# Stick-breaking heads taken two at a time, with the mask added by a matmul

## What is computed

```python
z = jnp.einsum('bhqd,bhkd->bhqk', qb, kh) * scale
valid = key_pos < qpos
log_keep = jnp.where(valid, jax.nn.log_sigmoid(-z), 0.0)
after = lax.cumsum(log_keep, axis=3, reverse=True) - log_keep
attn = jnp.where(valid, jnp.exp(jax.nn.log_sigmoid(z) + after), 0.0)
out = jnp.einsum('bhqk,bhkd->bhqd', attn, vh)
```

## Time and profile before

| | us |
|---|---|
| median of 3 runs | 1650.35 (1649.11 to 1651.74) |
| the profiled execution | 1655.24 |
| its span, first to last instruction | 1653.4 |
| TensorE busy | 1580.4 (96%) |
| VectorE busy | 1065.9 (64%) |
| ScalarE busy | 750.5 (45%) |
| Pool busy | 450.5 (27%) |

### The profile page before, as it was taken

One profiled execution on the slowest core, in us unless ns is written; L12 is line 12 of the kernel. 1 busy time (PEld: TensorE's weight loads), 2 busy tenths in 40 slices (PEclk: granted clock), 3 DMA queues, 4 the chain that ended last, 5 costly groups with the idle time before them and its releaser, 6 DMA issues. The chain is left out here.

```text
span 1653.4 us, 32293 instructions
## 1 busy us (share of the span) xinstructions
PE 1580.4 (96%) x11998; PEld 1514.0 (92%) x11998; DVE 1065.9 (64%) x1685; ACT 750.5 (45%) x1079; POOL 450.5 (27%) x180
## 2 busy tenths in 40 slices
PE   8999899998999998999999999999998899899997
PEld 7778899998999998888999999999998888899997
DVE  6233777755755549886875553655539886877863
ACT  5233555544544533246454443544443335554442
POOL 4224300053434410000244443334410000244452
PEclk9779999999999999899999999999999899999999
DMA  7212445662565534324455564556644333456563
GB/s 241 72 52 90 115 153 179 193 224 89 178 177 185 194 118 144 104 86 126 146 169 175 172 210 148 164 176 181 204 125 140 103 102 114 146 175 184 186 229 98
DMA packets 65834, 250.87 MB, mean 152 GB/s; under 512 B 7520, under 2 KB 8800, under 8 KB 65760
## 3 DMA queue, kind: packets, MB, share of 16 engines
q1 hardware_dynamic: 65760, 249.85, 49.1%
HBM read 248.77 MB, written 1.05 MB: 151 GB/s over the span
## 5 line engine op out<-in xcount | busy, mean ns | idle before, releaser
L335 POOL TENSOR_TENSOR wlo<-raw,whi 128x1024 fp32r<-128x1024 f32 (+1 forms) x168 | 442.7, 2637 | 1182.3 <-ACT whi L378 1182.3
L1131 PE MATMUL W<-xh,whi 128*128 128x272 f32 (+2 forms) x2416 | 708.8, 293 | 16.5 <-DVE wlo L664 13.4
L1133 PE MATMUL W<-xh,wlo 128*128 128x272 f32 (+2 forms) x2416 | 699.3, 289 | 0.0
L1132 PE MATMUL W<-xl,whi 128*128 128x272 f32 (+2 forms) x2416 | 697.8, 289 | 0.0
L378 ACT ACTIVATE whi<-raw 128x1024 fp32r<-128x1024 f32 (+1 forms) x439 | 483.5, 1107 | 138.1 <-PE W L1133 97.4
L1131 PEld LDWEIGHTS W<-xh,whi 128*128 128x128 f32 x2416 | 462.7, 192 | 25.2 <-issue 18.0
L1132 PEld LDWEIGHTS W<-xl,whi 128*128 128x128 f32 x2416 | 463.0, 192 | 0.5
L1133 PEld LDWEIGHTS W<-xh,wlo 128*128 128x128 f32 x2416 | 462.8, 192 | 0.0
L664 DVE TENSOR_TENSOR wlo<-raw,whi 128x1024 fp32r<-128x1024 f32 (+1 forms) x269 | 345.1, 1283 | 69.1 <-ACT whi L378 68.7
L1131 PE MATMUL W<-ah,whi 128*128 128x272 f32 (+2 forms) x1168 | 333.4, 285 | 8.7 <-DVE proj L1068 3.5
L1133 PE MATMUL W<-ah,wlo 128*128 128x272 f32 (+2 forms) x1168 | 332.2, 284 | 0.0
(11 more groups left out here) (159 smaller groups left out, 1083.6 us busy)
## 6 DMA issues: line engine op xcount, KB each, us to landing
raw<-in_w SPq DMA_DIRECT2D x359, 512.0 KB, 3.6
raw<-in_w SPq DMA_DIRECT2D x80, 704.0 KB, 4.1
h<-in_hT SPq DMA_DIRECT2D x4, 272.0 KB, 5.0
out<-h SPq DMA_DIRECT2D x4, 256.0 KB, 2.5
scr<-in_cst SPq DMA_DIRECT2D x1, 1000.0 KB, 9.2
cst<-in_cst SPq DMA_DIRECT2D x1, 408.0 KB, 6.6
prm<-in_prm SPq DMA_DIRECT2D x1, 180.0 KB, 8.7
m<-in_meta SPq DMA_DIRECT2D x1, 64.0 KB, 8.9
```

Source lines behind the costliest of these rows:

```text
L335: pool.tensor_tensor(wlo[:, j, 0:cols], raw[:, j, 0:cols], whi[:, j, 0:cols].bitcast(F32), ALU.subtract).then_inc(lo_ready[j], 1)
L1131: pe.matmul(out, whi[:, j, w], mh, start=start and k == 0, stop=False, skip_group_check=True)
L1132: pe.matmul(out, whi[:, j, w], ml, start=False, stop=False, skip_group_check=True)
L1133: ins = pe.matmul(out, wlo[:, j, w], mh, start=False, stop=stop and k == len(rhs) - 1, skip_group_check=True)
```

## The change

The eight heads become four pairs, one pair every four steps from step 14. Both heads of a pair have one pass each on ScalarE and VectorE, over 2 x 432 columns in two neighbouring PSUM banks (XP).

- `scores(c)`, step 14 + 4c: for each of the two banks first one fast matmul (identity by a constant with -1e30 at masked keys, 432 columns), then the three matmuls of each head, the two heads by turns: one on array rows 0 to 63, the other on 64 to 127.
- `soften(c)`, step 15 + 4c; `keeps(c)`, step 16 + 4c, is one pass, without the mask. `sums(c)`, step 16 + 4c, uses negated constants. `arguments` is gone; `weights(c)`, step 17 + 4c, reads PSUM. `values(c)`, step 17 + 4c, takes the heads by turns on columns 0 to 63 and 64 to 127.
- Taps: 4 a step before step 14, 6 from there on.
- The values are turned at step 12 and copied at steps 13 to 15.
- Pool makes the rounded copies of the identity and the mask once, at the start; the constants grow by 128 columns.

```diff
-for name, n in [("kpad", CC * 384), ("u", CC * (CONV_K - 1 + T)), ("y", CC * T), ("soft", SBW),
-                ("keep", SBW), ("attn", SBW)]:
+for name, n in [("kpad", CC * 384), ("u", CC * (CONV_K - 1 + T)), ("y", CC * T), ("keep", 2 * SBW),
+                ("attn", 2 * SBW)]:
     SC2[name] = (o, n)
     o += n
...
-        room = 0 if s < 2 else 4 if s < G_GLU else 5 if s % 2 or s <= SB_FROM else 6
+        room = 0 if s < 2 else 4 if s < SB_FROM else 6
...
-        cst = sb("cst", [P, 3 * P + SBW])
+        cst = sb("cst", [P, 4 * P + SBW])
+        identr, hider = sb("identr", [P, P], F32R), sb("hider", [P, SBW], F32R)
...
-        trige = cst[:, 2 * P:3 * P]
-        unseen = cst[:, 3 * P:3 * P + SBW]
+        minus_later, minus_ones = cst[:, 2 * P:3 * P], cst[:, 3 * P:4 * P]
+        hide = cst[:, 4 * P:4 * P + SBW]
...
-        soft, keep, attn = s2("soft"), s2("keep"), s2("attn")
+        keep, attn = (s2(x).rearrange("p (b n) -> p b n", b=2) for x in ("keep", "attn"))
...
-        X = [ctx.enter_context(nc.psum_tensor(f"X{i}", [P, 512], F32)) for i in range(4)]
+        XP = ctx.enter_context(nc.psum_tensor("XP", [P, 2, 512], F32))
+        X = [XP[:, 0, :], XP[:, 1, :]] + [ctx.enter_context(nc.psum_tensor(f"X{i}", [P, 512], F32))[:, :] for i in (2, 3)]
...
             for j in range(2, 4):
                 lo(0, j, S8)
+            pool.wait_ge(cst_landed, 16)
+            pool.tensor_copy(identr[:, :], ident).then_inc(hide_ready, 1)
+            pool.tensor_copy(hider[:, :], hide).then_inc(hide_ready, 1)
             los(N_QKV1 - 1, 1, K8A)
             los(N_WO, G_WO1, K8A)
             los(N_DN, G_DN1, K11)
...
             def mixer(g, l, p, t):
-                def soften(hd):
-
-                    n = 3 * (SB_H * l + hd)
-                    act.wait_ge(z_mm, SB_H * l + hd + 1)
-                    if hd:
-                        act.wait_ge(keep_ready, SB_H * l + hd)
-                    act.activation(soft, X[hd % 2][:, 0:SBW], ACT.Abs).then_inc(soft_step, 1)
+                def soften(c):
+
+                    n = 3 * (CC * l + c)
+                    act.wait_ge(z_mm, CC * l + c + 1)
+                    act.activation(keep, XP[:, :, 0:SBW], ACT.Abs).then_inc(soft_step, 1)
                     act.wait_ge(soft_step, n + 1)
-                    act.activation(soft, soft, ACT.Exp, scale=-1.0).then_inc(soft_step, 1)
+                    act.activation(keep, keep, ACT.Exp, scale=-1.0).then_inc(soft_step, 1)
                     act.wait_ge(soft_step, n + 2)
-                    act.activation(soft, soft, ACT.Ln, bias=1.0).then_inc(soft_step, 1)
-
-                def weights(hd):
-                    act.wait_ge(arg_ready, SB_H * l + hd + 1)
-                    act.activation(attn, attn, ACT.Exp).then_inc(attn_ready, 1)
+                    act.activation(keep, keep, ACT.Ln, bias=1.0).then_inc(soft_step, 1)
+
+                def weights(c):
+
+                    act.wait_ge(cum_mm, CC * l + c + 1)
+                    if c:
+                        act.wait_ge(o_mm, CC * l + c)
+                    act.activation(attn, XP[:, :, 0:SBW], ACT.Exp).then_inc(attn_ready, 1)
 
                 def out_hi(c):
-                    act.wait_ge(o_mm, SB_H * l + 2 * c + 2)
+                    act.wait_ge(o_mm, CC * l + c + 1)
                     act.activation(ah[:, c, :], X[2][:, 0:T], ACT.Copy).then_inc(o_hi, 1)
 
                 for s in range(4 * N_MIX):
-                    hd, late = divmod(s - SB_FROM - 1, 2)
-                    if not late and 0 <= hd < SB_H:
-                        soften(hd)
-                    if not late and 1 <= hd <= SB_H:
-                        weights(hd - 1)
-                    if not late and hd >= 3 and hd % 2:
-                        out_hi((hd - 3) // 2)
+                    c, phase = divmod(s - SB_FROM, 4)
+                    if phase == 0 and 1 <= c <= CC:
+                        out_hi(c - 1)
+                    if phase == 1 and 0 <= c < CC:
+                        soften(c)
+                    if phase == 3 and 0 <= c < CC:
+                        weights(c)
                     if s == LN_FROM + 3:
                         for c in range(CC):
                             act.wait_ge(ln_cent, CC * l + c + 1)
@@ -978,23 +984,10 @@
                             dve.scalar_tensor_tensor(y[:, c, :], u[:, c, k:k + T], w, y[:, c, :], ALU.mult,
...
-                def keeps(hd):
-
-                    n = SB_H * l + hd
-                    dve.wait_ge(soft_step, 3 * n + 3)
-                    if hd:
-                        dve.wait_ge(cum_mm, n)
-                    dve.scalar_tensor_tensor(keep, X[hd % 2][:, 0:SBW], 0.0, soft, ALU.max, ALU.add).then_inc(sp_step, 1)
-                    dve.wait_ge(sp_step, n + 1)
-                    dve.scalar_tensor_tensor(keep, unseen, 1.0, keep, ALU.subtract, ALU.mult).then_inc(keep_ready, 1)
-
-                def arguments(hd):
-
-                    n = SB_H * l + hd
-                    dve.wait_ge(cum_mm, n + 1)
-                    if hd:
-                        dve.wait_ge(o_mm, n)
-                    dve.scalar_tensor_tensor(attn, unseen, NEG, X[hd % 2][:, 0:SBW], ALU.mult, ALU.add).then_inc(arg_ready, 1)
+                def keeps(c):
+
+                    dve.wait_ge(soft_step, 3 * (CC * l + c) + 3)
+                    dve.scalar_tensor_tensor(keep, XP[:, :, 0:SBW], 0.0, keep, ALU.max, ALU.add).then_inc(keep_ready, 1)
 
                 def out_lo(c):
...
                     j, n = s % 4, 4 * g + s + 1
-                    hd, late = divmod(s - SB_FROM - 1, 2)
-                    if not late and 1 <= hd < SB_H + 1:
-                        arguments(hd - 1)
-                    if not late and 0 <= hd < SB_H:
-                        keeps(hd)
+                    pair, phase = divmod(s - SB_FROM, 4)
+                    if phase == 2 and 0 <= pair < CC:
...
                     else:
                         scaled(proj[:, GSB + s - G_QK, t:], j, n, t).then_inc(evac_done, 1)
                     lo_ahead(g + s // 4, j, K8D, K8D)
-                    if G_V + 2 < s <= G_V + 5:
-                        b = s - G_V - 3
+                    if G_V < s <= G_V + 3:
+                        b = s - G_V - 1
                         dve.wait_ge(v2_mm, 3 * l + b + 1)
...
                     taps(s)
-                    if not late and hd >= 3 and hd % 2:
-                        out_lo((hd - 3) // 2)
...
 
                 def attn_gate(j):
                     for m in (2 * j, 2 * j + 1):
@@ -1375,43 +1366,50 @@
 
...
             def mixer(g, l, t):
-                def scores(hd):
-
-                    c, p0, bank = hd // 2, 64 * (hd % 2), hd % 2
+                def scores(c):
+
                     pe.wait_ge(evac_done, 4 * g + G_V + 2 * c + 2)
-                    if hd == 1:
+                    if c == 0:
                         pe.wait_ge(v2_ready, 3 * l + 1)
-                    elif hd >= 2:
-                        pe.wait_ge(arg_ready, SB_H * l + hd - 1)
+                        pe.wait_ge(hide_ready, 2)
+                    else:
+                        pe.wait_ge(attn_ready, CC * l + c)
+                    for bank in range(2):
+                        mm(X[bank][:, 0:SBW], identr[:, :], hider[:, :], True)
                     for b in range(3):
                         a, w = P * b, T - P * b
-                        ins = mm(X[bank][:, SB_AT[b]:SB_AT[b] + w], kpad[p0:p0 + 64, c, a:a + P],
-                                 proj[p0:p0 + 64, QQ + c, a:T], b == 0)
+                        for bank in range(2):
+                            p0 = 64 * bank
+                            ins = mm(X[bank][:, SB_AT[b]:SB_AT[b] + w], kpad[p0:p0 + 64, c, a:a + P],
+                                     proj[p0:p0 + 64, QQ + c, a:T], False)
                     ins.then_inc(z_mm, 1)
...
-                def sums(hd):
-
-                    bank = hd % 2
-                    pe.wait_ge(keep_ready, SB_H * l + hd + 1)
-                    for b in range(3):
-                        for jb in range(b, 3):
-                            r = BLK[jb][1] - BLK[jb][0]
-                            w = T - P * jb
-                            ins = mm(X[bank][:, SB_AT[b] + P * (jb - b):SB_AT[b] + P * (jb - b) + w],
-                                     (trige if jb == b else ones)[0:r, :], keep[0:r, SB_AT[jb]:SB_AT[jb] + w], False)
+                def sums(c):
+
+                    pe.wait_ge(keep_ready, CC * l + c + 1)
+                    for bank in range(2):
+                        for b in range(3):
+                            for jb in range(b, 3):
+                                r = BLK[jb][1] - BLK[jb][0]
+                                w = T - P * jb
+                                ins = mm(X[bank][:, SB_AT[b] + P * (jb - b):SB_AT[b] + P * (jb - b) + w],
+                                         (minus_later if jb == b else minus_ones)[0:r, :],
```

(55 more changed lines are left out.)

## The result

| | before | after |
|---|---|---|
| median of 6 runs, us | 1648.27 | 1658.57 |
| ratio to before (95% interval) | | 1.0068 (1.005 to 1.0086) |
| profiled execution, us | 1655.24 | 1658.78 |
| its span, us | 1653.4 | 1656.9 |

A forecast was written before the change was run, and what follows sets the result against it. The prediction took TensorE to set the mixer's time, through its work, its waits for VectorE and its clock. Work and waits -6.6 us, clock +19.7, together +13.1 on 1650.35, gave 1663.5 us; range 1643 to 1677.

The forecast's parts named there:

- scores of a pair: TensorE in the mixer: two heads' scores side by side take 1.1 us, within bounds of 1.02 and 2.04.
- values of a pair: TensorE in the mixer: two heads' values side by side take 1.2 us, within bounds of 1.06 and 2.12.
- work per layer: TensorE's work in a layer's mixer: scores save 2.2 us and values 3.7, together 5.9 us less.
- wait at the turns: TensorE waits 2.0 us behind slab 12, before turning the values, until VectorE has evacuated slab 11.
- wait before the first sums: TensorE waits 4.0 us for VectorE's keeps before the first pair's sums, where it waited 0.6 before.
- before the second, the third: TensorE waits 2.4 us before each of these sums, with VectorE's L664 and 6 taps ahead of keeps.
- idle time, both layers: TensorE's waits in the mixers: per layer 11.2 us instead of 8.6.
- falls behind waits before sums: TensorE's clock falls at all three waits before sums in each layer: six falls of 5.0 us, 30 in all.
- clock, both layers: Half clock in the mixers: 30 us for six falls, less 10.3 for the present ones, is 19.7 more.
- Overlap: Two heads' scores and values run side by side on TensorE; rival without overlap: 1676 us, chance 0.17.
- step-through: Walk through the first layer's mixer with estimated lengths, giving TensorE waits of 0.3, 2.0, 4.0, 2.4, 2.4 and 0.1 us.
- the held clock: Rival: in the mixers the clock falls only at the 4.0 us wait, once a layer; 1643.5 us, chance 0.20.

The follow-up runs named there:

- e3: The kernel after with scores and values looped one head behind the other instead of by turns; 1672.53 us.
- e7: e5 without the two hide matmuls of each pair, so nothing is masked; 1607.30 us.
- e9: The kernel after, unchanged, profiled a second time; one execution of 1664.34 us.
- e2: The kernel after with the first three waits before sums filled with idle matmuls whose result is not used; 1632.56 us.
- e1: The kernel after with taps dealt 6, 0, 11, 8 in each four steps from step 14, instead of 6 a step; 1622.88 us.
- e4: The kernel after with the old deal of taps (5 a step from step 8 to 14, then 5 and 6 by turns); 1657.17 us.
- e10: The kernel after with a list of taps per step found by stepping through its queues; 1605.65 us.
- e6: The kernel before, single heads, with only its taps dealt anew by a list found by stepping through its queues; 1617.62 us.
- e5: The kernel after with taps dealt 3 a step in steps 2 to 11, 4 in 12 and 13, then 5, 0, 15, 8 in each four; 1610.01 us.

## Why the prediction was right

The forecast was 1663.5 us from 1650.35, +13.1; measured is +10.3. The time itself, 1658.57, is 4.9 us below the forecast: 2.8 of it are the change, and 2.1 the kernel before, whose median over six runs is 1648.27. Term by term:

| term | forecast | measured |
|---|---|---|
| scores of a pair | 1.1 us | 1.03 |
| hide of a pair | 0.40 | 0.49 |
| values of a pair | 1.2 | 1.07 |
| work per layer | -5.9 | -6.3 |
| wait at the turns | 2.0 | 2.15, 2.17 |
| wait before the first sums | 4.0 | 3.28, 3.72 |
| before the second, the third | 2.4, 2.4 | 2.31, 2.31; 2.53, 2.73 |
| before the fourth | 0.1 | 0, 0.25 |
| idle time, both layers | +5.2 | +4.0 |
| falls behind waits before sums | six at 5.0 | six at 4.5 |
| clock, both layers | +19.7 | +19.7 |

The work: 8 x 1.02 + 8 x 1.06 = 16.6 us a layer before, 4 x (1.03 + 0.49 + 1.07) = 10.4 now. The idle time is span less busy in the windows: 171.8 - 157.3 = 14.5 against 165.6 - 152.9 = 12.7 in the first layer, 16.7 against 14.5 in the second. The clock: in the first layer three groups of sums, start to start, take 7.9, 6.0 and 6.9 us instead of 4.4 each, and the slabs behind them 5.6, 4.6 and 5.3 instead of 3.2: 13.5 us, the same in the second layer. That is 27, with 3 for two falls that the sum had left out, less the 10.3 of before. The two are at the turns, which the prediction had in its range and not in its sum, and at 746.6 us, which it did not have at all. Together 27 + 3 - 10.3 = 19.7, and -12.6 + 4.0 + 19.7 = +11.1, within 0.2 of the 10.9 of the mixers. That the clock's term is the same to the tenth is luck: smaller falls, and two more of them.

Overlap: the choice near the lower end was right, and it was not safe from the rows. Its reason, that loads of weights and matmuls of one head mostly alternate, is not what rows 3 show: both fill the same 1.1 us from 701.7 on, side by side. So this term came out by luck as well, and e3 shows that it holds in full by turns only. The Trainium skill's sentence on parallel tiles (TensorEngine Tiling (Array Packing), Key Properties) agrees with 1.03 us for two heads. Its other sentence, that a change of tiling mode drains the engine, no run tests by itself. What the rows leave for it is small: scores start 0.49 us behind the start of hide, whose columns alone are 0.40, the slab follows scores without idle time, and in e7 the slab ahead of scores is 0.2 us longer than one ahead of a slab.

The waits: the step-through was right within 0.35 us but for the first sums. There 4.0 was 0.7 too long in the first layer and 0.3 in the second. The 0.44 us between the layers go with the fall at the turns, which holds TensorE up and shortens what it has to wait afterwards: in e9, where the clock falls at the turns of both layers, both waits are 3.28. Where the other 0.3 come from stays open. It changed nothing, since 3.28 is long enough for a fall.

The clock: that it falls at all six waits before sums was the step with the most doubt, and the runs bear it out both ways, with e2 (waits filled, no falls there) and e1 (the second and third waits gone, and the falls with them). What was mis-sized is the single fall, 5.0 against 4.5. It is 5.8 us at the first sums, where it sets in with them, and 3.0 and 4.5 at the second and third, where it sets in 2.4 and 1.3 us behind their start (up to 2.5 in the second layer). The forecast also took it for one in five that the clock holds at 2.4 us; in four profiles of pairs (after, e3, e4, e9) there are 24 groups of sums behind waits of 1.89 us or more, and it fell at every one.

The evidence that the prediction had for the held clock was weaker than it took it to be. It was one execution: the wait of 2.35 us at 215 us without a fall. The second profile of before has the same wait at 205.02, and there the clock does fall; and in the first one it had fallen behind a wait of 2.26 us at 830.89, slabs next, which the prediction leaves out (the last row):

```profile
205.02 0.39 PE L1131 MATMUL W<-xh,whi 128*128 128x258 f32 x1 [2.35 <-DVE wlo L664]
...
205.80:209.20 3.40, 3.40 (x19) 3.40 (x18) 3.09 (x6) 1.93 (x4) 0.00 (x0) 0.53 0.85 278
...
831.00:835.00 4.00, 4.00 (x20) 4.00 (x21) 2.78 (x4) 3.58 (x6) 2.05 (x1) 0.57 0.73 224
```

Over the twelve profiles of this case (two each of the kernels before and after, one of each other run) the clock fell behind this wait in 7, behind the one of 2.3 us at 830.89 in 10, behind the one of 2.5 at 1453.10 in 8. So ahead of slabs a wait of 2.3 to 2.5 us brings a fall in some executions and not in others, and ahead of the sums it did so each time. That the thin sums make the difference fits these counts, but no run changes only what follows the wait.

Of the 2.8 us by which the forecast is too high the idle time is 1.2 and the work 0.8; the other 0.8 is no more than the intervals leave open.

The prediction did not see that the same taps, dealt otherwise, turn the loss into a gain of 2 to 3%. The rows for it were there: VectorE's queue order made every wait it listed.

## What to carry to other kernels

When a pass on one engine feeds a wait on TensorE, look at what stands ahead of it in that engine's queue, not at how busy the engine is: here VectorE's load fell by 9.5 us a layer and TensorE waited longer, and moving the same 124 taps a layer gave 35 us. Price a wait of TensorE with the clock that it may cost: the two waits of 2.31 us cost 3.0 and 4.5 us more behind them, with thin fp32 matmuls next. And do not take one execution's clock behind a wait for a rule. Last, compare a new structure with the old one only after both have had their filler work dealt anew: the mixers of the kernel before and of e10 are 47 us apart (328.4 and 281.0), of which the new deal alone gave 33 (e6, 295.2) and the pairs 14.

## What the runs showed of the hardware

The clock can fall without any wait. In the kernel after, the fourth sums stand directly behind a slab and run at full clock; just behind them it is at half:

```profile
741.00:746.50 5.50, 5.50 (x35) 4.60 (x33) 2.56 (x4) 0.00 (x0) 0.00 (x0) 1.00 0.57 155
746.60:750.00 3.40, 3.40 (x14) 3.17 (x15) 1.94 (x5) 1.80 (x2) 0.00 (x0) 0.50 0.13 51
```

TensorE was busy all the time there, with 24 records of the sums, half of them only 16 columns wide. It is no single case: right behind sums that had not waited the clock also falls in e2 (733.8 us), e5 (719.7) and twice in e7 (700.1 and 720.5). Behind the waits of 2.3 to 2.5 us ahead of dense slabs a fall lasts 3.4 us in these profiles, ahead of sums 6.8 to 13.7, and in the kernel after the clock came back each time while slabs ran again.

Taken by turns, two heads' 64-row fp32 matmuls on separate rows and banks cost as much as one head's (1.03 against 1.02 us for six records a head), and 64-column ones on separate columns with different streams likewise (1.07 against 1.06). One head behind the other they take 1.59 and 2.12 (e3).
